# Holding back the gathers of the indexer's key pages: one page per unit of scores

## The reference

```python
def indexer_select(qi, wi, ki, qpos, topk):
    L = ki.shape[1]
    s = jax.nn.relu(jnp.einsum('bthd,bsd->bths', qi, ki))
    score = jnp.einsum('bths,bth->bts', s, wi)
    score = jnp.where(jnp.arange(L)[None, None, :] <= qpos[None, :, None], score, -jnp.inf)
    _, idx = lax.top_k(score, topk)
...
# attend_paged
    ki_past = pool_ki[page_table].reshape(db, n_past, IDX_DIM).astype(f32)
    ki_all = jnp.concatenate([ki_past, ki], axis=1)
    idx, valid = indexer_select(qi, wi, ki_all, qpos, topk)
```

## Time and profile before

| what | value |
|---|---|
| timed runs, us | 3273.46, 3274.58, 3277.65; median 3274.58 |
| span of the profiled execution, us | 3368.8 |
| TensorE busy, us | 2930.4 (87%) |
| VectorE busy, us | 1501.6 (45%) |
| ScalarE busy, us | 683.3 (20%) |
| GpSimd busy, us | 377.4 (11%) |

### The profile page before, as it was taken

The page is one execution under the profiler, slowest core; times in us unless marked ns, Lnnn a source line. Parts: engine busy times, 40 slices in busy tenths (PEclk is TensorE's granted clock), DMA queues, the critical chain, the costliest instruction groups (busy, mean ns, idle before and its releaser), DMA issues. The chain is left out here.

```text
span 3368.8 us, 38811 instructions
## 1 busy us (share of the span) xinstructions
PE 2930.4 (87%) x16567; PEld 2680.5 (80%) x16567; DVE 1501.6 (45%) x2009; ACT 683.3 (20%) x1091; POOL 377.4 (11%) x352
## 2 busy tenths in 40 slices
PE   3397999772687989999999979977788999999998
PEld 3285777562563989999999979955488999999997
DVE  4058999477541342323323253436534323233233
ACT  2042111024331121111111122222132111111110
POOL 3602112250213010000000000005101000000000
PEclk6598999885798989999999989976698999999999
DMA  4002222304214121121211111100011111211111
GB/s 147 25 7 72 93 92 72 135 33 161 76 40 128 60 60 42 40 55 39 57 38 38 44 24 44 46 15 18 29 51 44 51 44 38 57 38 54 41 38 64
DMA packets 207072, 189.49 MB, mean 56 GB/s; under 512 B 18220, under 2 KB 159664, under 8 KB 206762
## 3 DMA queue, kind: packets, MB, share of 16 engines
q1 hardware_dynamic: 198321, 163.58, 16.1%
q0 software_dynamic: 8576, 23.34, 2.3%
HBM read 153.30 MB, written 33.50 MB: 55 GB/s over the span
## 5 line engine op out<-in xcount | busy, mean ns | idle before, releaser
L1877 DVE TENSOR_TENSOR xt<-ps,xt 128x1056 f32<-128x1056 f32 x176 | 221.1, 1256 | 207.1 <-PE ps L1661 207.1
L1661 PE MATMUL ps<-ffn_high,f_whG 128*128 128x352 f32 x1056 | 230.1, 326 | 13.2 <-DVE ffn_low L1591 7.8
L1661 PE MATMUL ps<-f_hidh,f_whD 128*128 128x352 f32 x1056 | 230.0, 326 | 9.9 <-DVE f_wlD L1856 9.9
L1661 PE MATMUL ps<-ffn_high,f_wlG 128*128 128x352 f32 x1056 | 227.4, 323 | 3.3 <-issue 3.3
L1661 PE MATMUL ps<-f_hidh,f_wlD 128*128 128x352 f32 x1056 | 229.7, 325 | 0.0
L1661 PE MATMUL ps<-f_hidl,f_whD 128*128 128x352 f32 x1056 | 228.8, 325 | 0.0
L1661 PE MATMUL ps<-ffn_low,f_whG 128*128 128x352 f32 x1056 | 228.7, 325 | 0.0
L1661 PE MATMUL ps<-ffn_low,f_whU 128*128 128x352 f32 x1056 | 228.7, 324 | 0.0
L1661 PE MATMUL ps<-ffn_high,f_whU 128*128 128x352 f32 x1056 | 227.8, 324 | 0.0
L1661 PE MATMUL ps<-ffn_high,f_wlU 128*128 128x352 f32 x1056 | 226.6, 323 | 0.0
L678 PE MATMUL ps<-pe_wh,even_high 128*128 128x512 f32 (+1 forms) x504 | 200.4, 398 | 11.7 <-POOL pe_wl L708 11.7
(11 more groups left out here) (534 smaller groups left out, 4878.3 us busy)
## 6 DMA issues: line engine op xcount, KB each, us to landing
pe_w<-in_w_in_even_dram SPq DMA_DIRECT2D x7, 2048.0 KB, 8.2
proj<-pe_out SPq DMA_DIRECT2D x56, 256.0 KB, 2.0
ht_even<-in_w_gate_dram SPq DMA_DIRECT2D x22, 512.0 KB, 5.3
ht_even<-in_w_up_dram SPq DMA_DIRECT2D x22, 512.0 KB, 6.5
ht_even<-in_w_down_dram SPq DMA_DIRECT2D x22, 512.0 KB, 3.9
ht_odd<-in_w_gate_dram SPq DMA_DIRECT2D x22, 512.0 KB, 5.1
ht_odd<-in_w_up_dram SPq DMA_DIRECT2D x22, 512.0 KB, 6.3
ht_odd<-in_w_down_dram SPq DMA_DIRECT2D x22, 512.0 KB, 3.9
```

Source lines behind the costliest of these rows:

```text
L1661: last = pe.matmul(g.ps[0:out_rows, b0 + c, 0:THIRD], lhs, rhs[:, c * THIRD:(c + 1) * THIRD], start=(first and n == 0), stop=(final and n ...
L1877: dve.tensor_tensor(xv, g.ps[:, 3 * (m % 2):3 * (m % 2) + 3, 0:THIRD], xv, ALU.add).then_inc(added, 1)
```

## The change

Ahead of each page's two gathers GpSimd now waits until VectorE has weighted one more unit: page n for n + 1 units. There are 48 units and 32 pages, so the last page waits for unit 32, the end of the fourth of six query tiles.

```diff
@@ -404,6 +404,7 @@
                                ).then_inc(placed_rows, 1)
             pool.wait_ge(placed_rows, 2)
             for n in range(NB * NPAGE):
+                pool.wait_ge(weighted, n + 1)
                 for c in range(2):
                     pool.indirect_dma_start(out=pages[:, n, c, :], out_offset=None, in_=key_rows,
                                             in_offset=bass.IndirectOffsetOnAxis(ap=ids[:, n:n + 1], axis=0)
                                             ).then_inc(w_pages, 16)
```

## The result

The changed kernel takes 3319.88 us (median of 4 runs, 3313.26 to 3320.92) against 3274.23 us before: a ratio of 1.0131, with a 95% interval from 1.0117 to 1.0146, that is 38 to 48 us more. Forecast were 3321 us, slower.

The account below looks back on a forecast made before the run. The early gathers were held not to be the bound; delayed, they make TensorE 44.3 us late, plus 3 for its clock: 3274.6 + 47 = 3322 us. Forecast 3321, range 3273 to 3333.

Parts of the forecast that it names:

- The 67 us: TensorE's second projection, beside the gathers: 67.0 us lost to a stall in the profiled execution, absent from timed runs.
- Its cause: TensorE's stall at both gather bursts: trace writing blocked while GpSimd makes descriptors, 2.80 us per weight load and matmul.
- The mark that I had named: Profile after: stall moves to the scores, span grows 0 to 15 us, distance to timed median shrinks to 40 to 60.
- Rivals C and D: Projection stall real: C, it moves along, about 3276 us, chance 0.13; D, scoring escapes it, 3254 us, chance 0.13.
- Rival A: Gathers beside the scores: stall absent when timed, no or partial hold by VectorE, 3311 us; chance 0.21.
- The start: First gather at about 211.6, some 0.1 us behind the first unit's end; later waits never hold anything back.
- The pace: Page gathers at their own pace: 64 x 1.256 = 80.4 us as lower bound.
- The hold by VectorE: Gathers starting under two-SBUF-input accumulations wait for their end: cycle 1.6 us on average, TensorE 44.3 us late, not 33.6.
- VectorE pays nothing: VectorE's operations beside gathers: they aren't lengthened; subtractions kept 1.22 to 1.23 us.
- The landing: After the last gather's end: its traffic takes 1.65 us more before TensorE can start the pages.
- The clock: 32 page transposes after TensorE's idling run at 1.2 GHz: between 0 and 5 us more, taken as 3.
- The sum: End of the stage: 44.3 us late plus 3 for the clock, 47 us; without the hold 33.6 + 3 = 37.

Follow-up runs that it names:

- the first trace: The kernel before, unchanged, in the profiled execution the prediction read: span 3368.8 us against a timed median of 3274.58 us.
- Experiment 1: The kernel before, unchanged, traced again: 3277.07 us, span 3274.9; two more traced executions took 3280.93 and 3280.60 us.
- experiment 4: The changed kernel with VectorE's weighted sums reading one operand from PSUM, and TensorE waiting for VectorE before rewriting a bank: 3312.64 us, ratio 1.0108.
- experiment 2: The changed kernel with one wait, for the first weighted unit, in place of 32: 3317.51 us, ratio 1.0119.
- experiment 3: The changed kernel with one wait for all 48 units ahead of the first gather: 3360.01 us, ratio 1.0251.
- experiment 6: The changed kernel with GpSimd gathering only each page's first copy, SP loading the second by 32 plain DMAs: 3276.68 us, ratio 1.0006.
- experiment 7: The changed kernel with one wait in place of 32, for the fourth projection taken out, 21 us before the first unit: 3296.69 us, ratio 1.0057.
- experiment 8: The changed kernel, unchanged, run once more on the same chip as experiments 5 to 7: 3319.08 us, ratio 1.0129.
- the third trace of the kernel before: The kernel before, unchanged, in the first of two further traced executions after experiment 1's: 3280.93 us, span 3278.8.
- experiment 5: The kernel before with experiment 4's edit, weighted sums reading PSUM, as control: 3277.68 us against 3275.12 on the same chip, ratio 1.0007.
- the second set: The changed kernel repeated (experiment 8), 3319.08 us, beside the kernel before on the same chip, 3275.12 us.

## Why the prediction was right, step by step

*The 67 us are not in a timed run.* Right, and it decided the sign. The ground that counted was the arithmetic: a span 94 us above the timed median cannot be a timed run. Later executions gave the yardstick: a time lies 2.1 to 2.5 us above its span, so the first trace was some 97 us too long, against 88 found in two stalls.

*Its cause.* Wrong. "The writing of the trace, blocked while GpSimd makes descriptors" would have moved the stall into the scores. The even step of 2.80 us on which it was built is there from 115 to 154 us only, not from 90; from 91 to 115 the gaps are uneven. The mark that I had named failed: the span was to grow by 0 to 15 us and fell by 50; the distance to the timed median was to shrink from 94 to some 40 to 60 us and turned into 1.5 us the other way round. Neither the scores nor the second burst of gathers had a stall, and three of four traced executions of the kernel before had none. With both bursts hit in one execution and neither in others, something that lasted through that execution is likelier than chance at each burst; what it was is open, no run here brought it back. The back-pressure of the record path, of which the Trainium skill ("NOTIFIC — the notification-queue block", section 7.1) speaks, is thereby neither shown nor excluded: it can't be what gathers and traces alone bring about.

*Rivals C and D* rested on a stall that timed runs share. Experiment 1 removes both.

*Rival A* (no hold, 3311 us) is what experiment 4 made: 3312.64. Experiment 4 shows that the change itself has the holds.

*The start.* Right in kind: only the first wait holds (experiment 2). In size, the first gather came 147.11 - 146.23 = 0.88 us after the first unit's end, not 0.1.

*The pace.* 64 x 1.256 = 80.4 us, measured 80.2 to 80.4 (experiments 3 and 4).

*The hold by VectorE.* Right in kind (experiment 4), half in size: 85.8 - 80.1 = 5.7 us, not 10.7. The step that was mis-sized is "a cycle is 1.4 to 2.2, on average 1.6", and under it the rule that a gather which starts under such an operation always waits for its end. The first 22 cycles took (179.35 - 147.11) / 22 = 1.47 us, the next 14 (197.97 - 179.35) / 14 = 1.33. In the first 22 about every second gather isn't held. Two of VectorE's accumulations, and the gathers that start beside them:

```profile
161.21 0.88 DVE L563 SCALAR_TENSOR_TENSOR score<-ix_relu,ix_kw,score 128x640 f32<-128x640 f32 x1
163.18 0.90 DVE L563 SCALAR_TENSOR_TENSOR score<-ix_relu,ix_kw,score 128x640 f32<-128x640 f32 x1
```

```profile
161.37 1.55 POOL L409 DMA_INDIRECT ix_pg<-in_cache_kidx_dram,ix_ids  x1 [0.30 <-DVE score L563]
163.22 0.95 POOL L409 DMA_INDIRECT ix_pg<-in_cache_kidx_dram,ix_ids  x1 [0.30 <-issue]
```

The gather at 161.37 starts 0.16 us into the operation and is done 0.83 us after its end; that at 163.22 starts 0.04 us into one and runs through it in 0.95. The traces of experiments 2, 6, 7 and 8 have the same pattern: gathers that started up to 0.09 us into an accumulation took 0.95, those that started 0.10 us or more into one were done 0.8 to 0.9 us after its end (the first gather after its long wait, 0.95). (Beside the projections it isn't as clear: in the third trace of the kernel before a gather that began 0.04 us after a subtraction of VectorE, at 89.38, took 2.01.) By the prediction's own step a gather follows a held one 1.12 us after an operation's end. That is 0.04 us into the next but one where the accumulations come every 0.98 us, as in the third tile, so it passes there. In the fifth tile they come every 1.255 us (177.07, 178.32, 179.58) and a gather every 1.26, in the sixth every 1.39 and a gather of 1.08 plus 0.30 as often: each gather starts 0.1 to 0.3 us before an accumulation's end, is done 0.83 after it, and loses 0.13 us or nothing. All this is read from timelines; no experiment moved a gather against an accumulation by itself.

*"VectorE pays nothing"* holds for the accumulations. But the operation that opens a tile (L560, one SBUF input) took 1.00 us for 128x1024 beside gathers (0.97 in experiment 8), and 0.75 in experiment 3, where none ran. The scores last 51.4 us with the change, 50.6 in experiment 3. It costs nothing here, since the gathers end last.

*The landing* took 234.38 - 232.91 = 1.5 us, forecast 1.65.

*The clock.* Put at 3 us, measured as nothing that belongs to the change. The transposes did run at the lower level, a batch every 0.85 us. But from the first transpose to the end of VectorE's last copy are 7.35 us, against 7.27 in experiment 1's trace: before, VectorE was still at its last sum and copied the first batch only 2.4 us after TensorE had begun (the earlier trace rows show 2.15), now after 1.2. The prediction set the slower batches against the copies alone and left out this head start. From the first transpose to the next stage's first matmul are 31.13 us with the change, 29.70 before; these 1.4 us are four later matmuls, which in experiment 8's trace of the same kernel take what they took before (TensorE's timeline of the change, and of experiment 8):

```profile
250.75 3.36 PE L471 MATMUL ps<-ix_relu,ix_wsum 128*32 128x512 f32 x4 [1.46 <-ACT ix_relu L515]
```

```profile
249.96 1.90 PE L471 MATMUL ps<-ix_relu,ix_wsum 128*32 128x512 f32 x4 [1.46 <-ACT ix_relu L515]
```

The granted clock over the four was 0.56 there and 1.00 in experiment 8, where the whole stretch takes 29.64 us. The control of experiment 5 and the half of experiment 6, where TensorE didn't idle for the pages, have the four at 3.26 and 3.62 us: so it doesn't take that idling, and it changes between executions of one kernel.

*The sum.* TensorE starts the pages 234.38 - 193.06 - 1.20 = 40.1 us late (1.20 is by how much the first unit already was), forecast 44.3; with what comes behind, 40 to 41.5, forecast 47. In the terms of the sum: 5.0 us too much for the holds, 1.6 to 3 too much for the clock, 0.8 too little for the start. The medians differ by 45.7 us and, in the second set, 44.0, but their intervals (38 to 48 and 37 to 48) hold 41.5 as well; the spans of the three good traces of the kernel before and the two of the changed one are 39.6 to 44.5 us apart. The mechanism gave the forecast to within 6 us; that it came within 2 us of the median is luck.

## What to carry to other kernels

Compare the span with the timed median before anything else is read: a span far above it holds something that timed runs don't, and a change must not be credited with it. GpSimd's indirect DMAs have a length of their own, here 1.256 us each (0.95 and 0.30 ahead of it; those of the K and V pages in experiment 1's trace take 0.95 and 0.30 too), so such a row has a latest start: the moment of need less the number times that step, 193 - 82 = 111 us in experiment 1's trace, some us less for the holds; by this sum a delay ahead of it is free (not tried), and behind it each microsecond counts in full (experiment 7). Waits on a faster counter pace nothing; only the first one does.

## What the runs showed of the hardware

One traced execution of four of the same program had TensorE issue 28 matmuls from 91 to 152 us, for a long part one every 2.80 us, and lose some 88 us in all, at both bursts of GpSimd's gathers; the cause is open. A gather beside VectorE's operations with two SBUF inputs was stretched to as much as 2.01 us from 0.95 (the third trace of the kernel before). In five traces a gather that started less than 0.10 us into an accumulation of the scores was not. A row of gathers and a row of such operations fell into step where their periods were near each other. VectorE's one-input operation that opens a tile took 0.97 to 1.00 us beside gathers and 0.75 without.
